# A two-layer hybrid decoder: order of the projections ahead of the attention, and the engine that scales the norm rows

## What is computed

```python
proj = x @ w_in                                   # one projection for all head groups
log_f = log_sigmoid(fox_f + f_bias); c = cumsum(log_f)
# 6 forgetting heads (64 wide): scores q.k/8 + c_q - c_k, causal softmax, times v
# 4 differential heads (two maps of 32, v of 64): (softmax_1 - lam*softmax_2) v,
#   with ALiBi slopes, then RMS norm over each head, times norm_g and (1 - lam_init)
# 6 gating heads: u * (tril(w_s) @ LayerNorm(g) + b_s) in chunks of 128, u and g = gelu(z)
y = concat([y_fox, y_diff, y_sgu]) @ w_out
h = LayerNorm(ALPHA * h + y)
```

## Time and profile before

| | |
|---|---|
| three runs | 2048.38, 2052.26, 2054.08 us; median 2052.26 |
| the profiled execution | 2058.27 us, its span 2056.5 |
| mean granted TensorE clock | 0.976 |
| TensorE busy | 1950.1 us (95%) |
| VectorE busy | 1112.6 us (54%) |
| ScalarE busy | 703.3 us (34%) |
| GpSimd busy | 327.9 us (16%) |
| fill of a raw weight tile, issue to landing | 4.8 us (median) |
| one put to `stacks`, issue to landing | 1.7 us (median) |

### The profile page before, as it was taken

The page is one execution under the profiler, slowest core; times in us unless marked ns, Lnnn a source line. Parts: engine busy times, 40 slices in busy tenths (PEclk is TensorE's granted clock), DMA queues, the critical chain, the costliest instruction groups (busy, mean ns, idle before and its releaser), DMA issues.

```text
span 2056.5 us, 25255 instructions
## 1 busy us (share of the span) xinstructions
PE 1950.1 (95%) x9341; PEld 1632.3 (79%) x9341; DVE 1112.6 (54%) x1792; ACT 703.3 (34%) x1017; POOL 327.9 (16%) x291
## 2 busy tenths in 40 slices
PE   7999999997989999999999999999978899999996
PEld 6888888886777888888788888888867788888885
DVE  6444445562776653444584444546647765444446
ACT  4323322343434433333242222224335343233321
POOL 6000000333314400000150000003332252000002
PEclk9999999998979999999999999999989999999998
DMA  5223233226731323222322223231277132322221
GB/s 219 102 82 107 78 120 110 80 85 176 190 88 62 116 71 119 102 82 102 113 97 88 102 82 120 74 132 70 78 204 193 42 108 78 121 98 86 102 102 41
DMA packets 41922, 216.99 MB, mean 106 GB/s; under 512 B 8724, under 2 KB 9172, under 8 KB 17928
## 3 DMA queue, kind: packets, MB, share of 16 engines
q1 hardware_dynamic: 38984, 200.35, 27.9%
q0 software_dynamic: 2880, 15.90, 3.1%
HBM read 198.28 MB, written 17.93 MB: 105 GB/s over the span
## 4 chain that ended last, share of the span: by engine, by line
PE 80%; DVE 10%; issue 3%; DMA 2%; ACT 2%; SPq 2%; POOL 1%; DVEq 0%; ACTq 0%; POOLq 0%
PE bank L857 74%; PE bank L1020 2%; SPq L391 2%; DVE res L1283 1%; DVE nat L1431 1%; DMA whiD<-stacks 1%; DMA rawA<-in_a_w 1%; PE bank L1116 1%; PE bank L885 1%; DVE st L1307 1%; DVE hl L1358 1%; DVE hl L1542 1%; DVE wlam L1532 1%; PE bank L1104 1%; DVE negm L1515 1%
## 5 line engine op out<-in xcount | busy, mean ns | idle before, releaser
L857 PE MATMUL bank<-whiD,hl 128*128 128x512 f32 x1408 | 444.6, 390 | 5.6 <-DVE hl L1358 5.1
L1283 DVE SCALAR_TENSOR_TENSOR res<-bank,res 128x512 f32<-128x512 f32 x384 | 258.5, 688 | 171.0 <-PE bank L857 168.8
L857 PEld LDWEIGHTS bank<-whiD,hl 128*128 128x128 f32 x1408 | 264.3, 188 | 65.0 <-DVE hl L1358 8.1
L857 PE MATMUL bank<-xhi,whiA 128*128 128x512 f32 (+1 forms) x768 | 287.6, 374 | 10.3 <-DVE xlo L1262 10.3
L857 PE MATMUL bank<-xlo,whiA 128*128 128x512 f32 (+1 forms) x768 | 285.9, 372 | 0.0
L857 PE MATMUL bank<-xhi,wloA 128*128 128x512 f32 (+1 forms) x768 | 285.9, 372 | 0.0
L857 PE MATMUL bank<-wloD,hl 128*128 128x512 f32 x704 | 274.1, 389 | 0.0
L857 PE MATMUL bank<-xhi,whiB 128*128 128x512 f32 x704 | 273.9, 389 | 0.0
L857 PE MATMUL bank<-xlo,whiB 128*128 128x512 f32 x704 | 273.9, 389 | 0.0
L857 PE MATMUL bank<-xhi,wloB 128*128 128x512 f32 x704 | 273.9, 389 | 0.0
L857 PEld LDWEIGHTS bank<-xhi,whiA 128*128 128x128 f32 x768 | 145.5, 189 | 38.0 <-DVE xlo L1262 8.5
(11 more groups left out here) (177 smaller groups left out, 3146.8 us busy)
## 6 DMA issues: line engine op xcount, KB each, us to landing
rawA<-in_a_w SPq DMA_DIRECT2D x63, 1024.0 KB, 4.8
rawB<-in_b_w SPq DMA_DIRECT2D x54, 1024.0 KB, 4.8
rawD<-in_d_w SPq DMA_DIRECT2D x46, 1024.0 KB, 4.8
stacks<-hl SPq DMA_DIRECT2D x240, 64.0 KB, 1.7
whiD<-stacks POOLq DMA_DIRECT2D x10, 768.0 KB, 6.0
wloD<-stacks POOLq DMA_DIRECT2D x10, 768.0 KB, 6.0
gbr<-in_gb_row SPq DMA_DIRECT2D x7, 1024.0 KB, 6.4
out<-nat SPq DMA_DIRECT2D x4, 512.0 KB, 2.6
```

Of the source, the lines that this page charges most:

```text
L857: ins = t_.matmul(out_, a_, b_, start=(start and k == 1), stop=(stop and k == n), skip_group_check=check)
L1283: v.scalar_tensor_tensor(out=r, in0=bank[b][:, :], scalar=scale, in1=r, op0=ALU.mult, op1=ALU.add).then_inc(step, 1)
```

## The change

- Pair 0 is projected right behind `natural(0)`. `natural(1)` and `natural(2)` follow it; `natural(1)` does its B half first, with the cumulative sum (now in bank 4) between its halves, and `natural(2)` takes chunks 4, 5, 6, 0 to 3, 7. Natural projections 0 and 1 now use banks 0 to 3, and 2 uses 4 to 7. The gating product and `project(l, 1)` come last as before. The host lays out the A weights in the new order.
- Pair 0's split query and key are kept in the four quarters of `wloD` instead of `hl` (`stage`), and SP puts them ahead of the later fills.
- `query`, `key`, `split`, the gate's LayerNorm and `c_ok` are reordered on ScalarE and VectorE to suit; ScalarE does `query_half(1)` and `key_half(1)` ahead of the copies of `natural(2)`. GpSimd loads the stacks of pair 0 ahead of the low halves of pair 1's weights.
- The norm rows (`gbr`) are loaded earlier in SP's list and scaled by two `activation`s on ScalarE ahead of the attention; GpSimd's `scale_gain(3 * l + 2)` goes.
- The last RMS stage runs in step `k = 6` instead of `5` (`RMS_AT`).

The functions `query`, `key`, `query_half` and `key_half` are otherwise only moved up in the file. The core of the diff:

```diff
+A_NATS = [A_NAT, A_NAT + 2, A_NAT + 3]
+A_QKS = [A_NAT + 1] + [A_QK + b for b in range(1, BODIES)]
+
+NAT_ORDER = [None, [4, 5, 6, 7, 0, 1, 2, 3], [4, 5, 6, 0, 1, 2, 3, 7]]
+NAT_BANK = [0, 0, 4]
...
+RMS_AT = (2, 3, 4, 6)
...
+        stages = [[wlo["D"][:, i * S:(i + 1) * S] for i in range(4)], [qhi, qlo, khi, klo]]
...
-                for j in range(1, NPROJ):
-                    fill("A", l * A_ALL + A_NAT + j + 1)
-                    fill("B", l * B_ALL + B_NAT + j + 1)
-                fill("A", l * A_ALL + A_QK + 1)
...
+                def put_query(b):
+                    hi, lo = stage(b)[0:2]
                     sp.wait_ge(qk_ok, (l * BODIES + b) * 2 + 1)
-                    put(b, 0, (qhi, qhi, qlo), q_put)
...
+                    put(b, 0, (hi, hi, lo), q_put)
+
+                def put_key(b):
...
-                    put(b, 2, (khi, klo, khi), k_put)
+                    put(b, 2, (hi, lo, hi), k_put)
+
+                fill("A", l * A_ALL + A_NATS[1])
+                fill("B", l * B_ALL + B_NAT + 2)
+                put_query(0)
+                put_key(0)
+                fill("A", l * A_ALL + A_NATS[2])
+                sp.wait_ge(c_ok, l + 1)
+                for h in range(FOX_H):
+                    for j in range(2):
+                        sp.dma_start(stacks[h // 2 * 2, h % 2, STACK - 1:STACK, 2 + j, :],
+                                     brow[32 * j + h:32 * j + h + 1, :].bitcast(F32)).then_inc(c_put, 16)
+                fill("B", l * B_ALL + B_WO)
+                fill("A", l * A_ALL + A_QK + 1)
+                sp.wait_ge(res_ok, (3 * l + 2) * NT)
+                sp.wait_ge(x32_ok, (3 * l + 2) * 2 * NC)
+                norm_params(3 * l + 2)
+                fill("A", l * A_ALL + A_QK + 2)
+                for b in range(1, BODIES):
+                    put_query(b)
+                    put_key(b)
                     fill("A", l * A_ALL + A_QK + b + 2)
...
-                query_half(1)
-                key_half(1)
...
                 load_stack(0, 0)
                 load_stack(0, 1)
+                query_half(1)
+                key_half(1)
                 query_half(2)
                 key_half(2)
...
                 load_stack(BODIES - 1, 0)
-                scale_gain(3 * l + 2)
                 load_stack(BODIES - 1, 1)
...
+                act.wait_ge(used["A"], l * AU_ALL + A_NATS[0] + 1)
+                split("A", l * A_ALL + A_QKS[0])
...
-                    act.wait_ge(used["A"], l * AU_ALL + A_NAT + j + 1)
-                    split("A", l * A_ALL + A_NAT + j + 1)
+                    if j == NPROJ - 1:
+                        act.wait_ge(used["A"], l * AU_ALL + A_NATS[j] + 1)
+                        query_half(1)
+                        key_half(1)
                     act.wait_ge(used["B"], l * BU_ALL + B_NAT + j + 1)
                     if j < NPROJ - 1:
                         split("B", l * B_ALL + B_NAT + j + 1)
+                    act.wait_ge(used["A"], l * AU_ALL + A_NATS[j] + 1)
+                    if j == 1:
+                        split("A", l * A_ALL + A_NATS[2])
                     if j == 0:
...
-                        src = bank[t + 4 * (j % 2)]
+                        src = bank[t + NAT_BANK[j]]
...
-                    if j == 1:
-
+                        act.wait_ge(y_done, (l * Y_ALL + Y_WO) * 8 + AHEAD)
+                        query(0)
+                        act.wait_ge(used["A"], l * AU_ALL + A_QKS[0] + 1)
+                        split("A", l * A_ALL + A_NATS[1])
+                        key(0)
                         act.wait_ge(fneg_ok, l + 1)
...
                         act.wait_ge(gb_ok, NT * l + NT)
                         a.activation(ghi, nat[:, :, 0:SGU_W], ACT.Copy).then_inc(ghi_ok, 1)
...
+                        act.wait_ge(cum_done, l + 1)
+                        a.activation(brow[0:FOX_H, :], bank[4][0:FOX_H, :], ACT.Copy).then_inc(chi_ok, 1)
...
-                query_half(1)
-                act.wait_ge(used["B"], l * BU_ALL + B_NAT + NPROJ)
                 wo_half("B", l * B_ALL + B_WO, 0)
-                act.wait_ge(cum_done, l + 1)
-                a.activation(brow[0:FOX_H, :], bank[0][0:FOX_H, :], ACT.Copy).then_inc(chi_ok, 1)
+                wo_half("B", l * B_ALL + B_WO, 1)
                 act.wait_ge(sgu_done, (l + 1) * (SGU_H // 2))
-                query(0)
-                key(0)
-                key_half(1)
+                act.wait_ge(gbr_landed, 16 * (3 * l + 2) + 16)
+                for w in range(2):
+                    a.activation(gbr[:, w, :], gbr[:, w, :], ACT.Copy, scale=ALPHA).then_inc(rs_step, 1)
                 query(1)
                 query_half(2)
-                wo_half("B", l * B_ALL + B_WO, 1)
 
...
-                n = l * A_ALL + A_QK + b
+                n = l * A_ALL + A_QKS[b]
...
-                        if c == KHALF:
-                            pe.wait_ge(lo_ok["B"], n_b + 1 + AHEAD)
...
-                                          start=(c == 0), stop=(c == NC - 1))
-                        if c == KHALF - 1:
-                            ins.then_inc(used["A"], 1)
+                                          start=(i == 0), stop=(i == NC - 1))
...
+                    pe.wait_ge(nat_free["A"], l * 2 * NT + min(j, 1) * NT + AHEAD)
                     if halved:
...
+                    if j == 2:
+                        pe.wait_ge(nat_free["B"], l * NT + AHEAD)
+                        pe.wait_ge(qk_ok, l * BODIES * 2 + 2)
+                        pe.wait_ge(c_ok, l + 1)
+                    order = NAT_ORDER[j]
+                    pe.wait_ge(lo_ok["B"], n_b + 1 + AHEAD)
+                    for i, c in enumerate(order):
+                        if c == 0:
+                            if j == 1:
+                                cumulate()
+                            pe.wait_ge(lo_ok["A"], n_a + 1 + AHEAD)
+                        ins = chunk(i, c)
+                        if c == max(order, key=lambda c_: (c_ < KHALF, order.index(c_))):
+                            ins.then_inc(used["A"], 1)
+                        elif c == NC - 1:
+                            ins.then_inc(used["B"], 1)
+
+                def cumulate():
+
+                    pe.wait_ge(lf_ok, l + 1)
+                    for b in range(NT):
+                        ins = t_.matmul(bank[4][0:FOX_H, :], lf[:, b, :], since[:, (3 - b) * P:(3 - b) * P + S],
+                                        start=(b == 0), stop=(b == NT - 1))
+                    ins.then_inc(cum_done, 1)
 
                 natural(0, True)
+                for _ in project(l, 0):
+                    pass
                 natural(1)
                 natural(2)
 
-                pe.wait_ge(nat_free["B"], l * NT + NT + AHEAD)
...
-                for _ in range(NC):
-                    next(between)
-
                 pe.wait_ge(nat_free["A"], l * 2 * NT + 2 * NT + AHEAD)
-                pe.wait_ge(lf_ok, l + 1)
-                for b in range(NT):
-                    ins = t_.matmul(bank[0][0:FOX_H, :], lf[:, b, :], since[:, (3 - b) * P:(3 - b) * P + S],
-                                    start=(b == 0), stop=(b == NT - 1))
-                ins.then_inc(cum_done, 1)
-
                 pe.wait_ge(wslo_ok, l + 1)
...
-                for _ in between:
-                    pass
+                pe.wait_ge(nat_free["B"], l * NT + NT + AHEAD)
                 for _ in project(l, 1):
                     pass
...
-                split("A", l * A_ALL + A_NAT + 1)
+                split("A", l * A_ALL + A_QKS[0])
                 split("B", l * B_ALL + B_NAT + 1)
...
                 dve.wait_ge(gate_ok, l * NT + NT)
                 for t in range(NT):
                     v.bn_stats(gst[:, t, :], nat[:, t, 0:SGU_W]).then_inc(gst_ok, 1)
-                split("A", l * A_ALL + A_NAT + 2)
+                query(0)
                 dve.wait_ge(gst_ok, l * NT + NT)
                 wait_here(4)
                 for t in range(NT):
                     v.bn_aggr(gmv[:, t, :], gst[:, t, :]).then_inc(gmv_ok, 1)
                 dve.wait_ge(wshi_ok, l + 1)
                 v.tensor_tensor(wslo, wsr, f32(wshi), ALU.subtract).then_inc(wslo_ok, 1)
+                split("A", l * A_ALL + A_NATS[1])
+                key(0)
+                dve.wait_ge(fln_ok, l + 1)
+                v.scalar_tensor_tensor(out=lf[:, :, :], in0=flog[:, :, :], scalar=0.0, in1=fln[:, :, :],
+                                       op0=ALU.min, op1=ALU.subtract).then_inc(lf_ok, 1)
                 dve.wait_ge(grs_ok, l + 1)
                 for t in range(NT):
                     v.tensor_scalar(nat[:, t, 0:SGU_W], nat[:, t, 0:SGU_W], gmv[:, t, 0:1], grs[:, t:t + 1],
                                     ALU.subtract, ALU.mult).then_inc(gn_ok, 1)
-                split("B", l * B_ALL + B_NAT + 2)
                 for t in range(NT):
                     dve.wait_ge(gn_ok, l * NT + t + 1)
```

(37 more changed lines are left out.)

71 lines of the change are left out of this document (26 added, 45 removed).

## The result

The changed kernel takes 2023.0 us (median of 4 runs, 2022.58 to 2024.23) against 2053.17 (2048.38 to 2055.87) for the kernel before: a ratio of 0.9854, interval 0.984 to 0.9869. It is faster, by 30.2 us (1.5%), but 15 us slower than the forecast of 2008 and just outside its range of 1997 to 2020. The profiled execution took 2022.58, its span 2020.8.

What follows compares the result with a forecast made beforehand. TensorE, busy 95% of the span, was taken as the bound. Savings of 27.9 + 4.2 + 9.5 + 2.6 + 1.5 - 1.0 = 44.7 us from the median 2052.3 gave about 2008, range 1997 to 2020.

Steps and rivals of the forecast that it cites:

- The start of the attention: Mixer's front, both layers: projecting pair 0 earlier removes the wait for its stacks before the first score; 27.9 us saved.
- the one that was put at 0 to 0.5: Projection 1 waiting for banks 6 and 7 from natural projection 2, mostly covered by the gating product; cost 0 to 0.5.
- Rival 2: Mixer's front: VectorE's or ScalarE's queue late for natural projection 2 or projection 1, 3 to 6 us a layer; 2017, chance 0.15.
- rivals 4 and 5: Wait moves to pair 1's stack at step 8 (2045, chance 0.03); `query_half(1)`'s late fill makes it slower (2062, 0.02).
- The clock at the start: Attention steps 0 to 4 at the full clock, 9.0 us instead of 11.08; 4.2 us saved in both layers.
- The term against it: Early attention: steps 0 to 5 outrun SP's puts of pair 1, so the fill behind them is late; -1.0 us, both layers.
- The norm rows on ScalarE: Steps 28 to 32: without GpSimd's scaling the `wlam` stall and the half clock behind it go; 9.5 us saved.
- The RMS stage one step later: L1507 leaves the step where GpSimd makes the last A half's low part; its stall goes, 2.6 us saved.
- The low clock in steps 24 to 28: Low clock beginning right after the L1507 stall partly goes; 1.5 us taken of a possible 6.5.
- rival 3: Another stall brings the low clock on again in steps 24 to 32, only stalls are saved: 37.5 us, 2015; chance 0.15.
- projection 1 within 1 us: Sign for right, at the end of the mixer's front: projection 1 ends within 1 us of 481.6.
- L1507 four times at 0.28: Sign for right, in the RMS stage: VectorE's four norm-gain multiplications each take 0.28, with none held up.

Runs made afterwards that it cites:

- one of the last versions: Changed kernel with GpSimd waiting for the RMS stage, plus pair 4's key split taken first in step 24: 2005.93 us, ratio 0.9764.
- the very last: Changed kernel with GpSimd waiting for the RMS stage, pair 4's key split first in step 24, and the A fill amid pair 1's key puts: 2003.14 us.

## Why the prediction was right, and where it failed

**The start of the attention: right.** 27.5 of 27.9. The waits of the new order are the ones that were named, and the only one of TensorE in the new front is the one that was put at 0 to 0.5 (waits of TensorE in 395 to 482: total, times, longest):

```profile
PE bank L1050 <- DVE vals L1456: 0.5, 1, 0.5
```

Rival 2 needed late queues and didn't come. Nor did rivals 4 and 5: TensorE has no wait for a stack in the whole attention, and ScalarE's `query_half(1)` at 466.66 was released by TensorE and not by its fill. VectorE's timeline in the new front:

```profile
428.16 2.47 DVE L1285 TENSOR_TENSOR wloA<-rawA,whiA 128x2048 fp32r<-128x2048 f32 x1 [3.20 <-ACT whiA L656]
...
431.71 1.22 DVE L1476 SCALAR_TENSOR_TENSOR lf<-flog,fln 128x24 f32<-128x24 f32 x1 [0.48 <-ACT fln L796]
432.85 5.87 DVE L1480 TENSOR_SCALAR nat<-nat,gmv,grs 128x384 f32<-128x384 f32 x4
...
446.53 2.29 DVE L1285 TENSOR_TENSOR wloB<-rawB,whiB 128x2048 fp32r<-128x2048 f32 x1
```

The low part of B is done at 448.8 (446.53 + 2.29), inside the 446 to 449.4 that were given. The LayerNorm's four multiplications, 10.00 us in the earlier trace rows, take 5.87, and GpSimd's bias additions end at 437.7 (438 at worst was given).

**The clock at the start: right as a sum, by luck.** Two errors, of +1.1 and -0.7 us, nearly cancel. Steps 0 to 4 take 8.55 and 8.56 instead of the 9.0 assumed, a gain of 5.3 instead of 4.2 (in the second layer 2.7, above the bound of 2.6). The stretch at the start, once at 0.50:

```profile
480.00:485.00 5.00, 5.00 (x27) 4.22 (x26) 1.09 (x3) 1.89 (x5) 1.27 (x1) 1.00 0.55 141
```

The term against it was -1.0 and is -1.7 (11.67 and 11.09 for steps 4 to 8, against 10.52 and 10.53). Its cause is the one named, on ScalarE's timeline:

```profile
496.64 1.06 ACT L663 ACTIVATE whiA<-rawA 128x1024 fp32r<-128x1024 f32 x1 [2.19 <-DMA rawA<-in_a_w]
```

With the fill earlier this wait goes. Over the profiles the length of the wait and that of steps 4 to 8 go together: 0, 1.27, 1.72, 2.19 and 2.60 us of wait in the first layer have 10.56, 10.72, 11.19, 11.67 and 12.06 (the last is the version with the scaling back on GpSimd). SP issued it 8.0 us after the first score (490.43), 8.5 were forecast.

**The norm rows on ScalarE: right.** 9.5 predicted, 9.6 measured alone and 10.0 when undone. The 12.4 of the ledger holds 2.5 us that belonged to that one execution of before (38.1 us for steps 28 to 32 in it, 35.6 in the second profile).

**The RMS stage one step later: wrong, and this is the step that failed.** "The stall of 1.52 (1.54) goes, and 0.9 us of VectorE moves to a later step: 2.6; bounds 0 and 3.6." Instead of a gain of 2.6 the runs show a loss: 11.8 us alone, 10.2 beside the other two, outside the bounds and with the other sign. What was worked out holds for the place that was looked at: steps 20 to 24 shrink by 1.6 and 1.9 us (against the version with the stage in step 5). But `rms` runs behind both differential pairs, and the second place was never looked at. It could have been, in the trace of before. VectorE's last stage and GpSimd's next pair there, at the last pair of the first layer:

```profile
627.63 0.89 DVE L1507 TENSOR_TENSOR nat<-nat,mixr 128x128 f32<-128x128 f32 x4
```

```profile
630.36 4.74 POOL L555 TENSOR_TENSOR wloD<-rawD,whiD 128x1024 fp32r<-128x1024 f32 x2 [5.35 <-PE bank L1094]
```

The release in that bracket is the masking matmul of the last score: GpSimd starts its pair right behind step 39's score (629.58), 2.7 us after the stage has started and 1.8 after its end. A step here lasts about 2.5 us, so a stage one step later ends inside GpSimd's pair. And little is left behind the stage to hide a delay: pair 4 is the last, and the turn of Y (L1043) follows some 3 us behind the score of step 39 (632.62). The rule that explains it was cited in the prediction (the Trainium skill, "SBUF — State Buffer", section "Who interferes with whom": a VectorE instruction with two SBUF inputs and a GpSimd one that reads SBUF exclude each other). It was worked out for the mixer's front, and for the stage only at the place that the stage left.

**Both together.** The order and the scaling were forecast at 27.9 + 4.2 + 9.5 - 1.0 = 40.6, and with 1.5 of clock in steps 24 to 28 at 42.1; without the stage the change gains 39.4 (2052.17 to 2012.78), and the parts taken alone 28.3 + 9.6 = 37.9. They add up within 1.5 us.

**The low clock in steps 24 to 28: wrong, and small.** 1.5 was taken, -0.1 came; rival 3, "the low clock stays", was right about steps 24 to 28; for steps 28 to 32 it was wrong, they took 12.97 and 12.72 at the full clock. The stretches of the changed kernel still show it:

```profile
560.00:565.00 5.00, 4.16 (x17) 3.57 (x16) 3.82 (x11) 2.60 (x7) 0.00 (x0) 0.50 0.74 213
```

The L1507 stall is gone in this kernel (steps 20 to 24 take 10.53 and 10.65), so it wasn't what the low clock of these steps needs. What it needs stays open: it follows the wait of 2.1 us for the key here, and waits of 1.27 and 2.27 in one of the last versions, while in the profiled execution of the very last the same two waits have none behind them, and steps 24 to 28 take 14.4.

**The base.** The sum was made against the profiled 2058.3 and then taken whole from the median of 2052.3. But parts of the sum were the profiled run's own: the second profile of before (2051.51) is 4.4 us shorter in the attention, and it was this stretch from which "19.3 against 13.9" was read. The profiles give 35.7 between them, the medians 30.2; these 4.4 us are most of the 5.5 between the two. Of the 15.4 us by which the sum of 2007.6 missed, the stage makes 12.8 (2.6 promised, 10.2 lost). That leaves 2.6, of which the low clock of steps 24 to 28 makes 1.6; the last 1.0 is too small to be told from noise.

**Signs named ahead.** Of those for "right", no DMA wait at the first score, projection 1 within 1 us, clock 1.00 at the start, no `wlam` near 3.5, steps 28 to 32 near 14: all came. L1507 four times at 0.28 failed at the last pair, and it points straight at the fault. Of those for "wrong", the low clock around step 24 came, and the wait on `vals` in front of projection 1, with the 0.5 us that it was priced at.

## What to carry to other kernels

Before an instruction is moved on its engine, list every place at which it runs (each pair, each layer, the last pass above all), and at each of them what the engine that can hold it up (here GpSimd) does from the new start on; one place that improves says nothing about the others, and the last has the least behind it to hide a delay. Where two such instructions meet, let the one with time to spare wait: here a semaphore wait that cost GpSimd 0.8 us brought 14 to 15. Subtract from the median only what isn't peculiar to the profiled execution, which two profiles of the same kernel tell.

## What the runs showed of the hardware

- Four small multiplications (0.89 us together when alone) took 5.22 beside two GpSimd instructions of 2.4: single ones up to 2479 ns instead of 285. Taken one by one, the lines of the changed kernel show the order, VectorE's two long ones and GpSimd's two:

```profile
605.77 2.48 DVE L1542 TENSOR_TENSOR nat<-nat,mixr 128x128 f32<-128x128 f32 x1
608.17 2.42 DVE L1542 TENSOR_TENSOR nat<-nat,mixr 128x128 f32<-128x128 f32 x1
```

```profile
605.60 2.50 POOL L576 TENSOR_TENSOR wloD<-rawD,whiD 128x1024 fp32r<-128x1024 f32 x1 [5.35 <-PE bank L1124]
608.06 2.38 POOL L576 TENSOR_TENSOR wloD<-rawD,whiD 128x1024 fp32r<-128x1024 f32 x1
```

The first two multiplications pass (605.37 to 605.85). The third lasts as long as GpSimd's first subtraction, and the fourth, right behind it, as long as GpSimd's second: one VectorE instruction got through for each of GpSimd's. The second layer shows the same (its long ones start at 1597.98 and 1600.39, GpSimd's at 1597.82 and 1600.28). The measured price here is 4.3 us of VectorE, 3.0 of TensorE's waiting and 6.6 to 7.1 of time, once the clock is counted.
- A VectorE instruction doesn't have to be large to be held up: a `wlam` of 128x1 took up to 3487 ns instead of 219, and `lf` of 128x24 took 1.22 us beside GpSimd's bias additions, 0.17 in the profile of before.
- The clock fell in the profiled execution of one version and not in that of another behind the same two waits, 1.27 and 2.27 us. What a removed stall gives back beyond its own length is therefore known only within several us: steps 28 to 32 of the unchanged kernel took 19.32 in one execution and 16.96 in the other.
